# Two modulation groups of a diffusion-trunk kernel: from TensorE in the turnover to VectorE in the sub-layer before it

## The chip, the cores and the metric

One NeuronCore of a Trainium2 chip runs the whole program. The time is the device time of one execution in microseconds (us). Engines go by the profile's names: PE is TensorE (PEld its weight loads), DVE is VectorE, ACT is ScalarE, POOL is GpSimd, SP is SyncE, whose queue issues nearly all loads.

## The reference, cut to what matters

Two layers of a trunk, each of three sub-layers: SwiGLU, a token mixer, SwiGLU. Both token groups (128 prompt tokens, 256 latent tokens) go through all six sub-layers with shared weights. Every sub-layer is normed before and after and modulated by nine vectors a layer:

```
def adaln(cond, w, b):
    return (jax.nn.silu(cond) @ w + b)[:, None, :]
def pre_norm(x, mod, j, g):
    return rmsnorm(x, g) * (1 + mod_chunk(mod, 3 * j + 1)) + mod_chunk(mod, 3 * j)
def post_residual(x, out, mod, j, g, w):
    return x + w * mod_chunk(mod, 3 * j + 2) * rmsnorm(out, g)
def swiglu(h, w_in, w_out):
    gate, up = jnp.split(h @ w_in, 2, axis=-1)
    return (jax.nn.silu(gate) * up) @ w_out
```

`mod` is `silu(cond)` (two rows: prompt and latent) times a 1024 x 9216 matrix per layer, all float32. So there are 18 modulation groups of 1024 columns; sub-layer b uses groups 3b (shift), 3b+1 (scale) and 3b+2 (gate). D_MODEL is 1024, the inner width of SwiGLU 2816.

## The kernel before, in words

**Layout.** All activations stand transposed, features on the partitions, the 384 tokens in the columns: 8 tiles of 128x384 for the model width (KD = 8), 22 for the inner width. Every float32 product of the main matrices is made of three float32r matmuls (high x high, low x high, high x low), so each weight half of 1024x128 is split by ACT (WH, L394) and then by DVE (WL, L408) into its high and low part. Four such halves fit (the ring of WH and WL), and PE multiplies one after the other: `pe_half` (L439 to L441), 24 matmuls a half.

**The sub-layers.** Sub-layers 0 to 5 of the code (here: first to sixth) are ffn, even mixer, ffn, ffn, odd mixer, ffn. In an ffn, the in-phase takes 22 load slots of 256 columns (`in{s}`), the out-phase 12 (`out{s}`). Loads come in the order written out by `ring_order` (L129), six slots of 1 MB in RAW; SP waits until the slot's last user is done (`wait_ring`).

**The turnover.** Between two sub-layers PE sums squares over the partitions (L1616), DVE and ACT turn the sums into two scale rows, PE spreads them over the partitions (L1623, into bank 4 and bank 5), and then, for each of the 8 feature tiles, DVE scales the output (L1140), adds it to X (L1144), scales X (L1093) and takes the low part HL (L1107), with ACT giving the high part HH (L712) and the full one (L718). PE begins the next sub-layer with `pe_four` (L443 to L474): the first four halves at once, one feature tile after the other, each tile waiting for its HL. The first tile's eight matmuls on HH are L452 and L453, its four on HL L456, the other tiles L461 to L463, the last tile L470 to L472.

**Where the modulation groups come from.** A group is four load slots. There are two ways to compute one:

- On PE (`mod_pair`, L1536): 128 matmul records a group, straight from RAW, L1546, into a bank of its own. The turnover into sub-layer s+1 has one such group, named by `BETWEEN`: its first pair of slots is cut in pieces around the spread into bank 5, its second pair runs partly before and partly inside `first_four` (between the first and the second feature tile). After it ACT copies the rows out (`mod_rows_out`, L656, at the end of the turnover on ACT), PE transposes them (`mod_turn`, L1578, after the first four halves), ACT copies the columns (`mod_cols_out`, L661) and DVE adds bias and gain (`coefficients`, L1051).
- On DVE (`mod_sums`, L1079 and L1082): 16 multiply-add instructions of 128x256 a slot into SUMS or PARTS, within an ffn named in `SUMMED` (first, third and fourth sub-layer). PE then reduces each slot over the partitions with four matmuls between two halves (`mod_reduce`, L1600, 8 records), and for every two slots transposes a row (`sum_turn`, L1610, 2 records). Ten slots fall in the in-phase, those beyond ten in the out-phase after the output slots of `SUMMED_OUT` = (0, 1, 3, 4, 6, 7).

Before, the first sub-layer sums 4 groups (16 slots, six of them in its out-phase), the third and the fourth 3 groups each (12 slots, two of them in the out-phase).

Of the kernel before, what the change touches and what calls it, by code (L numbers as in the profile page):

```python
# [63 lines left out]

BETWEEN = ("modB", "modD", "modE", "modH", "modJ")
MOD_GROUPS = {"mod0": 2, "modA": 4, "modB": 1, "modC": 1, "modD": 1, "modF": 3, "modE": 1, "modG": 3, "modH": 1,
              "modJ": 1}


# [29 lines left out]


OPEN_BANK = (7, 6, 4, 7)
MOD_BANK = {6: 6, 7: 5, 8: 6, 12: 6, 16: 6, 17: 6}

IN_SLOTS = {"ffn": 22, "even": 16, "odd": 12}
OUT_SLOTS = {"ffn": 12, "even": 4, "odd": 4}
# [24 lines left out]
def ring_order():  # L132

    def run(st, a, b):
        return [(st, n) for n in range(a, b)]

    order = run("mod0", 0, 2) + run("in0", 0, 2) + run("mod0", 2, 8)
    for s in range(6):
        kind = SUBLAYERS[s][0]
        if s:  # L140
            order += run(f"in{s}", 0, 2) + run(BETWEEN[s - 1], 0, 4)
        if kind == "even":
            order += run(f"in{s}", 2, 6) + run("modC", 0, 2) + run(f"in{s}", 6, 7) + run("modC", 2, 4)
            order += run(f"in{s}", 7, 16) + run(f"out{s}", 0, 4)
        elif s in SUMMED:
            order += run(f"in{s}", 2, 4)
            for q in range(SUMMED_IN):
                order += run(f"in{s}", 2 * q + 4, 2 * q + 6) if q < 9 else run(f"out{s}", 0, 2)
                order += run(SUMMED[s], q, q + 1)
            for n in range(10):  # L150
                order += run(f"out{s}", n + 2, n + 3)
                q = SUMMED_IN + SUMMED_OUT.index(n) if n in SUMMED_OUT else None
                order += run(SUMMED[s], q, q + 1) if q is not None and q < summed_slots(s) else []
        else:
            order += run(f"in{s}", 2, IN_SLOTS[kind]) + run(f"out{s}", 0, OUT_SLOTS[kind])
    return order
# [23 lines left out]
def trunk(nc, x_prompt, x_sample, c, state_hgrn, cache_k, cache_v, c_ctx, mod_w, mod_b, norm_pre, norm_post,  # L180
# [5 lines left out]
    with ctx:  # L186
# [127 lines left out]
        rstd_done = sem("rstd_done")  # L314
# [306 lines left out]
        def _(act):  # L621
# [138 lines left out]
            def turnover(s, OUT, n):  # L760

                st = f"out{s}"
                nxt = ahead(act, split_act, s, "out", n)
                out_tile(s, OUT, st, n, 0, 6)
                nxt[0]()
                tile_squares(s, st, n, 1, 7)
                nxt[1]()
                if s == 5:
                    x_rows_out(0)
                    x_rows_out(1)  # L770
                    tile_scaled(s, OUT, 7)
                    root(sum_out(bank[0], 0), 0, (stat_done, 2 * s + 1))
                    for at in range(2, 2 * TOKS):
                        x_rows_out(at)
                    return
                root(sum_out(bank[0], 0), 0, (stat_done, 2 * s + 1))
                act.wait_ge(xy_done, 8 * s + 8)
                tile_scaled(s, OUT, 7)
                root(STAT[:, 4, :], 5, (sum_step, 5 * (s + 1)))
                high_parts(s + 1, 2)  # L780
                mod_rows_out(between(s + 1))

            def ffn(s):
                f, st = SUBLAYERS[s][1], f"in{s}"

                def pair(i, j):
                    nxt = [split_act(act, st, j + 2 + q, 8, i) for q in range(2)] if j < 20 else \
                        [split_act(act, f"out{s}", q, 8) for q in range(2)]
                    base = 22 * f + j
                    for b in range(2):  # L790
                        nxt[0][b]()
                        act.wait_ge(half_used, i * 12 + used(st, j, b))
                        act.wait_ge(gated, i * 6 + (base + b + 1))
                        act.activation(TT[:, b, :], cols3(bank[b]), ACT.Silu).then_inc(silu_done, 1)
                    nxt[1][0]()
                    nxt[1][1]()
                    for b in range(2):
                        act.wait_ge(gated, i * 6 + (2 + base + b + 1))
                        act.activation(AH[:, bass.ds(i * 6 + (j + b), 1), :], TT[:, 2 + b:3 + b, :],  # L799
                                       ACT.Copy).then_inc(act_hi, 1)  # L800
                    if s in SUMMED and j in (6, 10, 14, 18):
                        summed_rows_out(s, (j - 6) // 4)
                    if s in SUMMED and j in (8, 12, 16, 20):
                        summed_cols_out(s, (j - 8) // 4)

                ffn_pairs(act, pair, lambda: s and mod_cols_out(between(s)))
                for n in range(11):
                    for half in ahead(act, split_act, s, "out", n):
                        half()
                    if n == 0:  # L810
                        act.activation(STAT[:, 7, 1:2], EPSC[:], ACT.Sqrt)
                    if n in ROWS_OUT and 2 * ROWS_OUT[n] < summed_slots(s):
                        summed_rows_out(s, ROWS_OUT[n])
                    if n in COLS_OUT and 2 * COLS_OUT[n] < summed_slots(s):
                        summed_cols_out(s, COLS_OUT[n])
                    if n % 3 == 2:
                        for b in range(2):
                            out_tile(s, OUTF, f"out{s}", n, b, 2 * (n // 3) + b)
                turnover(s, OUTF, 11)
# [158 lines left out]
            def odd(s):  # L978
                for tau in range(24):
                    if tau % 2 == 0:  # L980
                        for half in ahead(act, split_act, s, "in", tau // 2):
                            half()
                    d = tau % 8
                    if tau < 16:
                        act.wait_ge(half_used, used(f"in{s}", tau // 2, tau % 2))
                        dst = (CB if tau < 8 else CG)[:, d, :]
                        for g, (t0, t1) in enumerate(GROUPS):
                            a = act.activation(dst[:, t0 + 1 + g:t1 + 1 + g], bank[tau % 4][:, t0:t1], ACT.Copy)
                        a.then_inc(proj_out, 1)
                    if tau == 3:  # L990
                        mod_cols_out(between(s))
                for d in range(KD):
                    act.wait_ge(conv_done, d + 1)
                    if d == 0:
                        act.wait_ge(half_used, used(f"in{s}", 11, 1))
                    for g, (t0, t1) in enumerate(GROUPS):
                        a = act.activation(HH[:, d, t0:t1], CG[:, d, t0 + 1 + g:t1 + 1 + g], ACT.Copy)
                    a.then_inc(cat_hi, 1)
                for n in range(3):
                    for b in range(2):  # L1000
                        ahead(act, split_act, s, "out", n)[b]()
                        out_tile(s, OUTC, f"out{s}", n, b, 2 * n + b)
                turnover(s, OUTC, 3)
# [19 lines left out]
        def _(dve):  # L1023
# [174 lines left out]
            def ffn(s):  # L1198
# [25 lines left out]
                    if s in SUMMED and j == 14:  # L1224
                        coefficients(first_group(SUMMED[s]))

                ffn_pairs(dve, pair, lambda: s and coefficients(between(s)))
                for n in range(11):
                    for half in ahead(dve, split_dve, s, "out", n):
                        half()  # L1230
# [194 lines left out]
            def odd(s):  # L1425
# [13 lines left out]
                for tau in range(24):  # L1439
                    if tau % 2 == 0:  # L1440
                        for half in ahead(dve, split_dve, s, "in", tau // 2):
                            half()
                    if tau == 3:
                        coefficients(between(s))
                    if tau < 16:
                        continue
                    d = tau - 16
# [73 lines left out]
        def _(pe):  # L1521
# [60 lines left out]
            def mod_reduce(s, q):  # L1582

                n0, k = summed_before(s) + q, q // 2
                if q % 2 == 0:
                    if n0 >= 4:
                        pe.wait_ge(sum_cols, n0 // 2 - 1)
                    if q == 0:
                        pe.wait_ge(out_done, 4 + 8 * s)
                    if q == 0 and s == 0:  # L1590
                        pe.wait_ge(open_cols, 4)
                    if q == 2 and s:
                        pe.wait_ge(mod_cols, between(s) + 1)
                    if q == SUMMED_IN:
                        pe.wait_ge(gated, 2 + 22 * SUBLAYERS[s][1] + 22)
# [31 lines left out]
            def first_four(s):  # L1627
# [6 lines left out]
                next(steps)  # L1634
                if s == 0:
                    open_turn(1)
                if s:
                    mod_pair(BETWEEN[s - 1], 2, range(2 if SUBLAYERS[s - 1][0] == "ffn" else 5, KD))
                for kk, _ in enumerate(steps, 1):
                    if s == 0 and kk in (1, 3):  # L1640
# [34 lines left out]
            def turnover(s):  # L1675
# [24 lines left out]
                     lambda t: sum_at(t, 0), closes=True).then_inc(stat_done, 1)  # L1700
                pe.wait_ge(rstd_done, 2 * s + 2)
                spread(bank[4], 1)
                st = BETWEEN[s]
                pe.wait_ge(out_done, 4 + 8 * s + 7)
                mod_pair(st, 0, range(early, early + 3))
# [5 lines left out]
            def ffn(s):  # L1711
# [17 lines left out]
                        if b == 0 and j in (8, 12, 16, 20) and s in SUMMED:  # L1729
                            sum_turn(s, (j - 8) // 4)  # L1730

                ffn_pairs(pe, pair, lambda: s and mod_turn(between(s)))
                st = f"out{s}"

                def quarter_pair(i, jj):
# [235 lines left out]

            def odd(s):
                first_four(s)
                mod_turn(between(s))
                for tau in range(4, 24):
                    if tau >= 20:
                        pe.wait_ge(conv_step, 4 * (tau - 20) + 1)
# [50 lines left out]
```

## Time and profile before

| what | us |
|---|---|
| median of 3 runs (1646.82 to 1647.25) | 1646.87 |
| the profiled execution, own time | 1645.01 |
| its span, first to last instruction | 1643.2 |
| PE busy | 1593.4 (97%) |
| DVE busy | 1067.7 (65%) |
| ACT busy | 693.2 (42%) |
| mean granted TensorE clock | 0.997 |

The page's engine table shows how busy an engine is over the whole program; which engine sets the time of a stretch is read from the chain of waits and from the timeline of the stretch. A matmul's record is longer than the step to the next one, since matmuls overlap. Durations of the timeline are of merged runs of equal instructions where a count stands behind.

### The profile page before, as it was taken

What the parts mean: (1) busy time and instruction counts of PE and PEld (TensorE: products, weight loads), DVE (VectorE), ACT (ScalarE), POOL (GpSimd) and SP (SyncE); (2) the same over time, 40 slices, a digit from 0 to 9 for tenths busy, and PEclk for the clock granted to TensorE, in tenths of its full rate; (3) what the DMA queues carried; (4) which work ended last, traced back from release to release, by engine and by line L of the source; (5) the groups of instructions that cost most, each with busy time, mean ns of one, the idle gap of its engine ahead of it and who ended that gap; (6) DMA issues with size and microseconds to landing.
All of it is one profiled execution on the core that took longest, in us unless ns stands there. A gap on an engine that the chain in (4) does not pass through costs nothing.

```text
span 1643.2 us, 25603 instructions
## 1 busy us (share of the span) xinstructions
PE 1593.4 (97%) x10383; PEld 1535.1 (93%) x10383; DVE 1067.7 (65%) x1950; ACT 693.2 (42%) x1228; POOL 42.1 (3%) x48
## 2 busy tenths in 40 slices
PE   5999999999999999999999999999999999999999
PEld 4999999988778989999999999999999999999999
DVE  5677778773568887777764777776472776343332
ACT  3433334463563466333343633333463356333333
POOL 2000000001100000000000000000000000000000
PEclk8999999999999999999999999999999999999999
DMA  9765556566221235555554655555363335333321
GB/s 329 248 196 168 192 169 216 179 219 207 86 81 35 91 117 184 190 177 180 191 168 128 205 168 192 179 173 185 129 206 129 128 108 183 125 125 122 116 71 38
DMA packets 255685, 260.12 MB, mean 158 GB/s; under 512 B 6625, under 2 KB 253826, under 8 KB 255570
## 3 DMA queue, kind: packets, MB, share of 16 engines
q1 hardware_dynamic: 250528, 253.25, 47.7%
q0 software_dynamic: 928, 2.44, 0.6%
q10 hardware_dynamic: 4114, 2.84, 0.6%
q8 instruction: 80, 1.31, 0.3%
q14 instruction: 35, 0.29, 0.1%
HBM read 255.88 MB, written 2.62 MB: 157 GB/s over the span
## 4 chain that ended last, share of the span: by engine, by line
PE 86%; DVE 7%; ACT 3%; issue 2%; POOL 1%; DMA 1%; ACTq 0%; DVEq 0%; POOLq 0%
PE bank L439 25%; PE bank L441 25%; PE bank L440 25%; PE bank L461 1%; PE bank L1616 1%; PE bank L463 1%; PE bank L462 1%; ACT WH L394 1%; DVE X L1144 1%; PE bank L1600 1%; DVE HL L1107 1%; DVE WL L408 1%; DVE SUMS L1409 1%; POOL WL L408 1%; DMA MIX<-in_x_sample 1%
## 5 line engine op out<-in xcount | busy, mean ns | idle before, releaser
L408 DVE TENSOR_TENSOR WL<-RAW,WH 128x1024 fp32r<-128x1024 f32 (+1 forms) x335 | 400.5, 1198 | 470.4 <-ACT WH L394 469.8
L394 ACT ACTIVATE WH<-RAW 128x1024 fp32r<-128x1024 f32 (+1 forms) x344 | 357.7, 1044 | 623.8 <-PE bank L441 610.6
L439 PE MATMUL bank<-HH,WH 128*128 128x384 f32 x1664 | 565.9, 340 | 8.0 <-DVE WL L408 3.5
L440 PE MATMUL bank<-HL,WH 128*128 128x384 f32 x1664 | 559.7, 336 | 0.0
L441 PE MATMUL bank<-HH,WL 128*128 128x384 f32 x1664 | 559.7, 336 | 0.0
L439 PEld LDWEIGHTS bank<-HH,WH 128*128 128x128 f32 x1664 | 313.3, 188 | 16.6 <-issue 10.7
L440 PEld LDWEIGHTS bank<-HL,WH 128*128 128x128 f32 x1664 | 313.3, 188 | 0.0
L441 PEld LDWEIGHTS bank<-HH,WL 128*128 128x128 f32 x1664 | 313.2, 188 | 0.0
L439 PE MATMUL bank<-AH,WH 128*128 128x384 f32 x704 | 238.5, 339 | 0.0
L440 PE MATMUL bank<-AL,WH 128*128 128x384 f32 x704 | 236.8, 336 | 0.0
L441 PE MATMUL bank<-AH,WL 128*128 128x384 f32 x704 | 236.7, 336 | 0.0
L1082 DVE SCALAR_TENSOR_TENSOR SUMS<-RAW,COND,SUMS 128x256 f32<-128x256 f32 x420 | 176.2, 478 | 0.0
L439 PEld LDWEIGHTS bank<-AH,WH 128*128 128x128 f32 x704 | 132.5, 188 | 2.0 <-ACT OUTF L747 1.0
L440 PEld LDWEIGHTS bank<-AL,WH 128*128 128x128 f32 x704 | 132.6, 188 | 0.0
L441 PEld LDWEIGHTS bank<-AH,WL 128*128 128x128 f32 x704 | 132.5, 188 | 0.0
L799 ACT ACTIVATE AH<-TT 128x384 fp32r<-128x384 f32 x88 | 45.6, 519 | 108.8 <-DVE TT L1216 108.8
L461 PE MATMUL bank<-HH,WH 128*128 128x384 f32 x192 | 66.7, 347 | 4.5 <-DVE HL L1107 2.9
L463 PE MATMUL bank<-HH,WL 128*128 128x384 f32 x192 | 64.7, 337 | 0.0
L462 PE MATMUL bank<-HL,WH 128*128 128x384 f32 x192 | 64.6, 337 | 0.0
L712 ACT ACTIVATE HH<-TT,MOD,CA 128x128 fp32r<-128x128 f32 x96 | 47.3, 540 | 33.6 <-DVE TT L1093 32.1
L1082 DVE SCALAR_TENSOR_TENSOR PARTS<-RAW,COND,PARTS 128x256 f32<-128x256 f32 x140 | 56.3, 478 | 0.0
L1221 DVE TENSOR_TENSOR AL<-TT,AH 128x384 fp32r<-128x384 f32 x88 | 48.8, 554 | 5.5
(241 smaller groups left out, 1496.3 us busy)
## 6 DMA issues: line engine op xcount, KB each, us to landing
RAW<-in_ffn_w_in SPq DMA_DIRECT2D x88, 1024.0 KB, 5.1
RAW<-in_mod_w SPq DMA_DIRECT2D x72, 1024.0 KB, 5.1
RAW<-in_ffn_w_out SPq DMA_DIRECT2D x32, 1024.0 KB, 5.2
RAW<-in_ab_w_in SPq DMA_DIRECT2D x16, 1024.0 KB, 5.7
RAW<-in_ffn_w_out SPq DMA_DIRECT2D x16, 768.0 KB, 4.9
RAW<-in_cv_w_in SPq DMA_DIRECT2D x12, 1024.0 KB, 5.1
RAW<-in_ab_w_out SPq DMA_DIRECT2D x4, 1024.0 KB, 5.2
RAW<-in_cv_w_out SPq DMA_DIRECT2D x4, 1024.0 KB, 5.4
```

Source lines behind the costliest of these rows:

```text
L394: e.activation(WH[:, (2 * m + b) % 4, 0:nk, :], RAW[:, p, 0:nk, b * P:(b + 1) * P], ACT.Copy).then_inc(half_hi, 1)
L408: e.tensor_tensor(WL[:, k, 0:nk, :], RAW[:, p, 0:nk, b * P:(b + 1) * P], WH[:, k, 0:nk, :].bitcast(F32), ALU.subtract).then_inc(half_ready, 1)
L439: e.matmul(out, WH[:, k, kk, :], xh(kk), start=(first and kk == 0), stop=False)
L440: e.matmul(out, WH[:, k, kk, :], xl(kk), start=False, stop=False)
L441: mm = e.matmul(out, WL[:, k, kk, :], xh(kk), start=False, stop=(last and kk == nk - 1))
L461: e.matmul(outs[b], WH[:, kh[b], kk, :], HH[:, kk, :], start=False, stop=False)
L462: e.matmul(outs[b], WH[:, kh[b], kk, :], HL[:, kk, :], start=False, stop=False)
L463: e.matmul(outs[b], WL[:, kh[b], kk, :], HH[:, kk, :], start=False, stop=False)
L712: a = act.activation(HH[:, d, t0:t1], TT[:, d % 2, t0:t1], ACT.Identity, bias=MOD[:, 24 * s + d, g:g + 1], scale=CA[:, s, d, g:g + 1])
L799: act.activation(AH[:, bass.ds(i * 6 + (j + b), 1), :], TT[:, 2 + b:3 + b, :], ACT.Copy).then_inc(act_hi, 1)
L1082: x = dve.scalar_tensor_tensor(a[:, g, :], w, by, a[:, g, :], ALU.mult, ALU.add)
L1221: dve.tensor_tensor(AL[:, at, :], TT[:, 2 + b:3 + b, :], AH[:, at, :].bitcast(F32), ALU.subtract).then_inc(act_ready, 1)
```

## The change

`modE` (group 12) leaves the turnover from third to fourth sub-layer and becomes the fourth group of `modF`, summed in the third sub-layer; `modH` (group 16) leaves the turnover from fourth to fifth and becomes the fourth group of `modG`, summed in the fourth. `BETWEEN` becomes a dictionary of the turnovers that still have a group (0, 1 and 4), and everything that belongs to such a group is left out elsewhere. In these two turnovers PE then only sums and spreads.

```
-BETWEEN = ("modB", "modD", "modE", "modH", "modJ")
-MOD_GROUPS = {"mod0": 2, "modA": 4, "modB": 1, "modC": 1, "modD": 1, "modF": 3, "modE": 1, "modG": 3, "modH": 1,
+BETWEEN = {0: "modB", 1: "modD", 4: "modJ"}
+MOD_GROUPS = {"mod0": 2, "modA": 4, "modB": 1, "modC": 1, "modD": 1, "modF": 4, "modG": 4,
                "modJ": 1}
-MOD_BANK = {6: 6, 7: 5, 8: 6, 12: 6, 16: 6, 17: 6}
+MOD_BANK = {6: 6, 7: 5, 8: 6, 17: 6}
@@ ring_order
-            order += run(f"in{s}", 0, 2) + run(BETWEEN[s - 1], 0, 4)
+            order += run(f"in{s}", 0, 2) + (run(BETWEEN[s - 1], 0, 4) if s - 1 in BETWEEN else [])
@@ ACT, turnover
-                mod_rows_out(between(s + 1))
+                if s in BETWEEN:
+                    mod_rows_out(between(s + 1))
@@ ACT, ffn
-                ffn_pairs(act, pair, lambda: s and mod_cols_out(between(s)))
+                ffn_pairs(act, pair, lambda: s - 1 in BETWEEN and mod_cols_out(between(s)))
@@ ACT, odd
-                    if tau == 3:
-                        mod_cols_out(between(s))
@@ DVE, ffn
-                ffn_pairs(dve, pair, lambda: s and coefficients(between(s)))
+                ffn_pairs(dve, pair, lambda: s - 1 in BETWEEN and coefficients(between(s)))
@@ DVE, odd
-                    if tau == 3:
-                        coefficients(between(s))
@@ PE, mod_reduce
-                    if q == 2 and s:
+                    if q == 2 and s - 1 in BETWEEN:
@@ PE, first_four
-                if s:
+                if s - 1 in BETWEEN:
                     mod_pair(BETWEEN[s - 1], 2, range(2 if SUBLAYERS[s - 1][0] == "ffn" else 5, KD))
@@ PE, turnover
                 spread(bank[4], 1)
+                if s not in BETWEEN:
+                    pe.wait_ge(out_done, 4 + 8 * s + 7)
+                    pe.wait_ge(rstd_done, 2 * s + 3)
+                    spread(bank[5], 6)
+                    return
@@ PE, ffn
-                ffn_pairs(pe, pair, lambda: s and mod_turn(between(s)))
+                ffn_pairs(pe, pair, lambda: s - 1 in BETWEEN and mod_turn(between(s)))
@@ PE, odd
                 first_four(s)
-                mod_turn(between(s))
```

## Rows read from the trace of the kernel before

**Rows 1.** The page: the chain that ended last, shares of the span by engine.

```profile
PE 86%; DVE 7%; ACT 3%; issue 2%; POOL 1%; DMA 1%; ACTq 0%; DVEq 0%; POOLq 0%
```

**Rows 2.** Chain of waits, turnover to the fourth sub-layer: start, us, what.

```profile
905.68 0.10 DVE STAT L1087
...
912.44 0.55 DVE HL L1107
```

**Rows 3.** Timeline of PE, 903.9 to 914 us: start, us, instruction, idle before.

```profile
904.91 0.86 PE L1546 MATMUL bank<-RAW,COND 128*32 128x128 f32 x24
905.82 0.94 PE L1623 MATMUL bank<-IDENT,STAT 128*128 128x128 f32 x6
906.69 1.74 PE L1546 MATMUL bank<-RAW,COND 128*32 128x128 f32 x56
908.74 0.41 PE L452 MATMUL bank<-HH,WH 128*128 128x384 f32 x1 [0.32 <-ACT HH L712]
...
911.25 1.52 PE L1546 MATMUL bank<-RAW,COND 128*32 128x128 f32 x48
913.05 0.45 PE L461 MATMUL bank<-HH,WH 128*128 128x384 f32 x1 [0.27 <-DVE HL L1107]
```

**Rows 4.** Timeline of PE, turnover to the fifth sub-layer.

```profile
1207.74 0.44 PE L461 MATMUL bank<-HH,WH 128*128 128x384 f32 x1 [0.28 <-DVE HL L1107]
```

**Rows 5.** Timeline of all engines, end of the turnover, 918 to 934 us.

```profile
926.16 0.34 PE L472 MATMUL bank<-HH,WL 128*128 128x384 f32 x1
...
926.41 0.37 ACT L656 ACTIVATE ROWS<-bank 128x256 f32<-128x256 f32 x1
...
926.67 1.05 ACT L394 ACTIVATE WH<-RAW 128x1024 fp32r<-128x1024 f32 x1
...
927.90 0.51 PE L1578 MATMUL bank<-IDENT,ROWS 128*128 128x8 f32 x4
...
929.20 0.42 PE L439 MATMUL bank<-HH,WH 128*128 128x384 f32 x1 [0.80 <-DVE WL L408]
```

**Rows 6.** Chain of waits, end of the turnover to the fifth sub-layer.

```profile
1221.01 0.19 PE bank L472
...
1221.28 0.99 ACT WH L394
```

**Rows 7.** Timeline of PE, tenth reduction and first sums: first, then third sub-layer.

```profile
240.61 0.43 PE L1600 MATMUL bank<-SUMS,PICK 128*32 128x128 f32 x8
...
324.44 0.76 PE L1616 MATMUL bank<-ONES,SUMS 128*128 128x44 f32 x6
...
819.57 0.43 PE L1600 MATMUL bank<-SUMS,PICK 128*32 128x128 f32 x8
...
900.68 0.54 PE L1616 MATMUL bank<-ONES,SUMS 128*128 128x44 f32 x4
```

**Rows 8.** Busy time there: stretch, length, PE, PEld, DVE, ACT, POOL, clock, DMA.

```profile
240.60:324.40 83.80, 83.80 (x521) 80.91 (x521) 69.61 (x142) 32.98 (x64) 0.00 (x0) 1.00 0.62 201
819.40:900.70 81.30, 81.30 (x487) 80.04 (x486) 45.73 (x76) 32.54 (x60) 0.00 (x0) 1.00 0.48 156
```

**Rows 9.** Timeline of PE around one reduction, first sub-layer.

```profile
256.09 0.34 PE L440 MATMUL bank<-AL,WH 128*128 128x384 f32 x1
256.26 0.34 PE L441 MATMUL bank<-AH,WL 128*128 128x384 f32 x1
...
256.89 0.45 PE L439 MATMUL bank<-AH,WH 128*128 128x384 f32 x1
```

**Rows 10.** Timeline of PE in the opening.

```profile
21.04 0.94 PE L1623 MATMUL bank<-IDENT,STAT 128*128 128x128 f32 x6 [1.87 <-DVE STAT L1087]
...
27.35 3.64 PE L1561 MATMUL bank<-RAW,COND 128*32 128x128 f32 x64 [5.24 <-DMA RAW<-in_mod_w]
```

**Rows 11.** Stretches: the opening (columns of rows 8); fifth sub-layer, PE alone.

```profile
15.00:50.00 35.00, 27.27 (x326) 24.34 (x318) 25.43 (x52) 17.49 (x36) 10.85 (x6) 0.85 1.09 348
...
1306.50:1309.90 3.40, 0.77 (x5) 1.00 0.00 0
```

## The prediction

> **What bounds the kernel now.** I read the page's chain that ended last first: PE holds 86% of it [rows 1], so PE's time counts wherever PE doesn't wait. Where it does wait is then a question for each stretch that the change touches, and there are two kinds. In the out-phases of the first and third sub-layers PE is busy for every microsecond of the stretch, at the full clock, while DVE has 14 us or more free of 81 to 84 [rows 8]: there each instruction added to PE lengthens the program, and work added to DVE costs nothing as long as it fits. In the turnovers it is the other way round. PE's sums end, DVE and ACT make two scale rows, and then DVE's elementwise chain over the feature tiles sets the pace: the chain of waits goes through DVE's reciprocal, the spread, and DVE's instructions up to HL of the second tile [rows 2]. PE's timeline has the group's matmuls exactly in those waits: after the third block of them it still sits idle for 0.27 us until HL is there, after the second for 0.32 us until ACT has HH [rows 3]. The turnover to the fifth sub-layer ends in the same wait, 0.28 us [rows 4].
>
> **Taken out of the turnovers.** Per turnover, PE loses 24 + 56 + 48 = 128 records, 0.86 + 1.74 + 1.52 = 4.12 us [rows 3], and the transposition of the rows, 0.51 us [rows 5]: 4.63 us of PE work, 9.26 us for both. What of it lay on the path?
> - First block, 904.91 to 905.77: the spread behind it begins at 905.82 [rows 3], and DVE's reciprocal, whose piece of the chain ends at 905.78, lets it go [rows 2]. With the block gone the spread still begins at 905.82. Gain 0.
> - Second block, until 908.4: the next matmul waits for ACT's HH, with 0.32 us idle [rows 3]. Gain 0, and PE waits some 2 us instead.
> - Third block, until 912.77: the next matmul follows 0.06 us after HL ends (912.44 + 0.55 = 912.99) [rows 2, 3]. Gain 0. From there PE runs the remaining tiles without a further wait, as before. The same holds for the turnover to the fifth sub-layer by its own row [rows 4].
> - ACT's copy of the rows, 0.37 us, stands just ahead of the first split of the next half, on which PE waits 0.80 us at 929.20 [rows 5]. The copy is on the path in form, but that split also waits until PE has let go of the weights: PE's matmul ends at 926.16 + 0.34 = 926.50. In the other turnover, where ACT is idle before it, the split begins 0.08 us after such an end, at 1221.28 after 1221.01 + 0.19 [rows 6]. So it could begin at 926.58 and begins at 926.67 [rows 5]: I take a gain of 0.09 us, with bounds 0 and 0.37.
> - In the turnover to the fifth sub-layer the split is let go by PE itself [rows 6]; the removed copy of the rows was over before. Gain 0.
> - PE's transposition, 927.90 to 928.41, lies in the wait that ends at 929.20 [rows 5]: 0. ACT's copy of the columns and DVE's two small instructions come after it, beside PE's full halves: 0. If that cover went, they would cost under 1 us together.
> - SP: the four loads of each group leave the place between slots 2 and 3 of the next sub-layer, so the next weight slots come earlier; no split waits for a load there, before or after.
>
> **Put into the out-phases.** The third and fourth sub-layers get four more summed slots each, 12 to 15: four reductions and two transposed rows on PE, four slots of DVE work, four loads in SP's queue, one more group of coefficients. The first sub-layer already runs this very program with 16 slots, so its out-phase is the price list. From the tenth reduction to the first sums it takes 324.44 - 240.61 = 83.83 us, the third sub-layer takes 900.68 - 819.57 = 81.11 us [rows 7] (the fourth the same 81.11, by the same view). The difference is **2.72 us** for four reductions and two rows. As a cross-check, one reduction: between L441 and the next L439 lie 0.63 us where the step from L440 to L441 is 0.17 [rows 9], so 0.46, and the first matmul behind it is 0.1 us slow (0.45 us where the others take 0.34): 0.56. Four of these are 2.2 us, two rows take the rest, 0.25 us each.
>
> DVE gets 69.61 - 45.73 = 23.9 us more in each out-phase and then stands at 69.6 of 83.8 us [rows 8]. In the first sub-layer PE is busy for all of those 83.80 us, so the later splits are still in time; the loads too, which SP issues behind the same waits for DVE. The last slot is summed after the eighth of twelve output slots, well ahead of the turnover. If DVE's cover were gone, each late split would show as a wait of PE's L439 for L408.
>
> **The sum.** 2 x 2.72 - 0.09 = **+5.35 us**. For the profiled execution that is 1645.01 + 5.35 = 1650.4; the median of before stands 1.86 us above that execution (1646.87), so the median becomes **1652.2 us**, +0.33%. Bounds: the removed work returns between 0 and 0.37 us for ACT's copy, and up to 0.3 us a turnover if PE's idle between matmul blocks also held up the waiting matmul; on the other side a first matmul after idle takes 0.41 to 0.45 us instead of 0.34 [rows 3], two or three times a turnover, up to 0.3 us. With one of the two ends at a time that gives 1651.3 (5.35 - 0.28 - 0.6) to 1652.9 (5.35 + 0.09 + 0.6).
>
> **Rivals.**
> - **Faster: the group's matmuls did hold up PE.** The place is the turnover; if the waits shown after the blocks are only the time in which a full queue of small matmuls runs empty, then all 4.63 us leave the path and 2.72 come back: -1.91 each, 1646.87 - 3.8 = 1643.1 us. It decides from the point where PE's step before L461 shortens with nothing ahead of it, that is, if more than 2.72 of the 4.63 us were exposed. Against it: in both turnovers the matmul starts 0.05 to 0.1 us after DVE's HL ends [rows 2, 3], and DVE waits for nothing of PE's there but the spreads. 5%.
> - **The same: about half is hidden.** If the turnovers give back over 1 us each, or the reductions fall into waits, the sum stays below 3.3 us: about 1649. The first sub-layer's 2.72 us speak against it; what speaks for it is only that four small instructions may be placed luckier. 7%.
> - **The clock falls.** In the new turnover PE works 0.94 us, waits 2 us, works 2 us on the first tile, and waits 1.8 us. In the opening PE had waited 1.87 us, run a spread of 0.94 us and begun a wait of 5.24 us [rows 10] when the granted clock fell to 1.2 GHz; the mean of 0.85 over 35 us [rows 11] makes 35 x 0.15 / 0.5 = 10.5 us at the low level. Once per turnover this costs up to 5.2 us less the 1.8 us that PE would have waited: some 3.4 to 5.2 each, 1659 to 1663 us in all. Against it: around the 2.99 us hole of the fifth sub-layer PE was busy for 0.77 of 3.40 us and kept the full clock [rows 11], and the new turnover is busier than that. 6%.
> - **DVE comes late** in the fuller out-phases, or SP's loads do. Each late split costs up to its own 1.2 us; with one per added slot, 8 x 1.2 = 9.6, about 1661 us. The first sub-layer's full PE row [rows 8] speaks against it. 3%.
> - That the change doesn't do what it says (matmuls left in the turnovers) I hold for excluded by the diff: the calls are behind the new conditions.
>
> [...]
>
> **Numbers.** Forecast 79%, clock 6%, DVE 3%, same 7%, faster 5%. A measurement of this kernel can tell about 0.2%, 3.3 us, from no change. Faster 0.05; same 0.09 (the case and the low tail of the forecast); slower 0.86. The range takes the forecast's bounds, a microsecond for the gap between the profiled execution and the median, and a part of the neighbouring cases on both sides: 1649.8 to 1655.0.
>
> **What would show it.** In the profile of after: no L1546 and L1578 in these two turnovers; first sums to the first L439 as long as before within 0.1 us (900.68 to 929.20 us in the first of them [rows 5, 7]); waits of the spread L1623, L452 and L461 longer, with DVE and ACT as releasers; tenth reduction to first sums 83.8 us in the third and fourth sub-layers, DVE at 70 us there; clock 1.00 throughout. I am wrong if the turnovers shorten by more than 0.5 us each, if L439 waits for L408 in the out-phases, or if the clock column shows less than 1.00 there.

## The result

The changed kernel takes 1653.44 us (median of 7 runs, 1650.59 to 1653.55) against 1646.82 before: ratio 1.0039, 95% interval 1.0028 to 1.0049. It is slower by 6.6 us, 0.40%. Of the seven runs of the kernel before, one took 4680.29 us; the other six lie between 1645.08 and 1647.25 us, and without it their median would be 1646.81. The forecast was 1652.2 us in a range of 1649.8 to 1655.0, and slower with a chance of 0.86.

The page of the changed kernel (1652.87 us for the profiled execution, 7.9 us over that of before): PE has 192 instructions less and as much busy time, DVE 47.6 us more.

```profile
span 1651.1 us, 25359 instructions
...
PE 1594.7 (97%) x10191; PEld 1534.5 (93%) x10191; DVE 1115.3 (68%) x2078; ACT 693.5 (42%) x1232; POOL 42.2 (3%) x48
```

The out-phase of the third sub-layer, from the windows view of the changed kernel (columns as in [rows 8]). It now reads like the first sub-layer's of before: 83.80 us, PE busy in all of it, DVE at 69.

```profile
820.50:904.30 83.80, 83.80 (x521) 80.89 (x521) 69.34 (x141) 32.99 (x64) 0.00 (x0) 1.00 0.62 202
```

The turnover behind it on PE, from the timeline of the changed kernel. It answers to [rows 3]: from the first spread to the second, to the first tile and to the second tile the steps are as before to 0.1 us, and where the group's matmuls were PE is idle, 0.93, 1.98 and 1.72 us. New is what comes next: L461, 0.34 us long before, takes 0.52 us in the two rows ahead of the last.

```profile
907.72 0.94 PE L1620 MATMUL bank<-IDENT,STAT 128*128 128x128 f32 x6
909.59 0.91 PE L1620 MATMUL bank<-IDENT,STAT 128*128 128x128 f32 x6 [0.93 <-DVE STAT L1086]
912.47 0.42 PE L452 MATMUL bank<-HH,WH 128*128 128x384 f32 x1 [1.98 <-ACT HH L712]
...
916.78 0.44 PE L461 MATMUL bank<-HH,WH 128*128 128x384 f32 x1 [1.72 <-DVE HL L1106]
...
918.27 0.52 PE L461 MATMUL bank<-HH,WH 128*128 128x384 f32 x1
919.23 0.52 PE L461 MATMUL bank<-HH,WH 128*128 128x384 f32 x1
...
934.27 0.42 PE L439 MATMUL bank<-HH,WH 128*128 128x384 f32 x1 [1.07 <-DVE WL L408]
```

The clock column says why. Windows of 2 us in the changed kernel (the column behind POOL is the granted clock, share of full speed): it falls to 0.50, that is 1.2 GHz, within 916 to 918 us, when the second tile's matmuls (from 916.78) have just begun, and is back between 920 and 922; in the next turnover it falls between 1210 and 1212.

```profile
914.00:916.00 2.00, 1.05 (x5) 0.65 (x4) 1.93 (x6) 0.58 (x2) 0.00 (x0) 1.00 0.01 4
916.00:918.00 2.00, 1.22 (x6) 1.22 (x7) 1.93 (x5) 1.71 (x4) 0.00 (x0) 0.88 0.03 8
918.00:920.00 2.00, 2.00 (x8) 2.00 (x7) 1.93 (x5) 1.75 (x5) 0.00 (x0) 0.50 0.00 0
920.00:922.00 2.00, 2.00 (x11) 2.00 (x10) 1.97 (x4) 1.75 (x5) 0.00 (x0) 0.77 0.00 0
...
1210.00:1212.00 2.00, 0.92 (x3) 0.92 (x4) 1.87 (x5) 0.98 (x2) 0.00 (x0) 0.76 0.91 313
1212.00:1214.00 2.00, 2.00 (x8) 2.00 (x7) 1.97 (x6) 0.98 (x2) 0.00 (x0) 0.50 0.03 8
```

Where the 7.9 us between the two profiled executions lie, by the first sums (L1616, L1613 in the changed kernel) and the first L439 behind them in each timeline:

| stretch | before | after | difference |
|---|---|---|---|
| start to the first turnover's sums | 324.44 | 324.59 | +0.15 |
| from there to the second turnover's sums (even mixer) | 281.10 | 281.90 | +0.80 |
| from there to the third turnover's sums | 295.14 | 297.86 | +2.72 |
| third turnover, first sums to first L439 | 28.52 | 29.92 | +1.40 |
| from there to the fourth turnover's sums | 266.18 | 268.89 | +2.71 |
| fourth turnover, first sums to first L439 | 28.44 | 28.51 | +0.07 |
| from there to the end of the span | 419.4 | 419.4 | 0.0 |

The out-phases bring 5.43 us, the turnovers 1.47. Both bare turnovers had a stretch of 3.4 us at the low clock, and yet one cost 1.40 us and the other 0.07. In the third turnover the low stretch fell on the second and third feature tile, behind which PE has no wait in which to make the time good. In the fourth it fell on the first tile, and that tile has a wait behind it: PE waits 0.61 us for the second tile, where it waited 1.72 us in the third turnover, and the rest goes on as before.

```profile
1211.08 0.69 PE L452 MATMUL bank<-HH,WH 128*128 128x384 f32 x1 [1.78 <-ACT HH L712]
...
1215.59 0.44 PE L461 MATMUL bank<-HH,WH 128*128 128x384 f32 x1 [0.61 <-DVE HL L1106]
```

The 0.80 us of the even mixer, which the change doesn't touch, goes with the clock too: it was low between 524 and 530 us in this execution and not in the one of before. In a row of 21 runs of the kernel before the mean clock read 0.995 to 0.997 and the time 1645.3 to 1648.8 us. So the kernel before probably has such falls as well, though its one profile shows none behind the opening.

### The profile page after: what moved, and what is told of

Read it like the earlier page. It is cut to its first block, busy times and chain, and to the rows that moved or that the text cites. A ratio compares the mean times of both kernels' runs of the same rounds, so it can differ in the third digit from the quotient of the medians.

```text
span 1651.1 us, 25359 instructions
## 1 busy us (share of the span) xinstructions
PE 1594.7 (97%) x10191; PEld 1534.5 (93%) x10191; DVE 1115.3 (68%) x2078; ACT 693.5 (42%) x1232; POOL 42.2 (3%) x48
## 4 chain that ended last, share of the span: by engine, by line
PE 87%; DVE 6%; ACT 2%; issue 2%; DMA 1%; SPq 1%; DVEq 0%; ACTq 0%
PE bank L439 25%; PE bank L441 25%; PE bank L440 24%; PE bank L461 1%; PE bank L462 1%; PE bank L463 1%; PE bank L1613 1%; PE bank L1597 1%; ACT WH L394 1%; DMA RAW<-in_mod_w 1%; SPq L532 1%; DVE X L1143 1%; PE bank L1911 1%; DVE WL L408 1%; DVE SUMS L1408 1%
## 5 line engine op out<-in xcount | busy, mean ns | idle before, releaser
L439 PE MATMUL bank<-HH,WH 128*128 128x384 f32 x1664 | 566.2, 340 | 8.6 <-DVE WL L408 3.7
L441 PE MATMUL bank<-HH,WL 128*128 128x384 f32 x1664 | 559.8, 336 | 0.0
L439 PEld LDWEIGHTS bank<-HH,WH 128*128 128x128 f32 x1664 | 313.3, 188 | 17.7 <-issue 11.2
L441 PEld LDWEIGHTS bank<-HH,WL 128*128 128x128 f32 x1664 | 313.2, 188 | 0.0
L439 PE MATMUL bank<-AH,WH 128*128 128x384 f32 x704 | 239.6, 340 | 0.0
L441 PE MATMUL bank<-AH,WL 128*128 128x384 f32 x704 | 236.7, 336 | 0.0
L439 PEld LDWEIGHTS bank<-AH,WH 128*128 128x128 f32 x704 | 132.4, 188 | 3.6 <-ACT OUTF L747 1.8
L441 PEld LDWEIGHTS bank<-AH,WL 128*128 128x128 f32 x704 | 132.4, 188 | 0.0
L1081 DVE SCALAR_TENSOR_TENSOR PARTS<-RAW,COND,PARTS 128x256 f32<-128x256 f32 x252 | 101.3, 478 | 0.0
L461 PE MATMUL bank<-HH,WH 128*128 128x384 f32 x192 | 67.2, 350 | 6.2 <-DVE HL L1106 4.7
```

The lines of the kernel that those rows point to most:

```text
L439: e.matmul(out, WH[:, k, kk, :], xh(kk), start=(first and kk == 0), stop=False)
L441: mm = e.matmul(out, WL[:, k, kk, :], xh(kk), start=False, stop=(last and kk == nk - 1))
L461: e.matmul(outs[b], WH[:, kh[b], kk, :], HH[:, kk, :], start=False, stop=False)
L1081: x = dve.scalar_tensor_tensor(a[:, g, :], w, by, a[:, g, :], ALU.mult, ALU.add)
```

## The experiments

Medians against runs of the kernel before on the same chip. The kernel before had 1646.8 us beside all of them, but 1646.0 beside the last two.

**1. Filler in the two bare turnovers.**

```
+            def fill(n):
+                for kk in range(n):
+                    for strip in range(4):
+                        pe.matmul(bank[6][32 * strip:32 * strip + 32, 0:P], COND[:, kk % KD, :], ONES[:],
+                                  start=True, stop=True)
...
                     pe.wait_ge(out_done, 4 + 8 * s + 7)
+                    fill(3)
                     pe.wait_ge(rstd_done, 2 * s + 3)
                     spread(bank[5], 6)
+                    fill(7)
                     return
...
+                elif s:
+                    fill(6)
```

> The changed kernel with filler in the two turnovers without a group: 12, 28 and 24 matmuls (24, 56 and 48 records, as many as the group had there) of constant data into bank 6, whose results nobody reads. Theory: the changed kernel loses 2 x 2.7 us in the out-phases and a further 1 to 2 us because the granted clock falls for a few us in the bare turnovers. Then the filler keeps the clock at 1.00 there, the turnover to the fourth sub-layer (first sums to first L439) goes back from 29.92 to about 28.5 us, and the median lands at 1652.2 us, 1 to 1.4 below the changed kernel's 1653.4. Rival, the longer turnover comes from something else that left with the group (order of the loads, ACT's start): it stays at 29.9 us and the median at 1653.4. Rival, small matmuls hold PE up: over 1654.

Measured: 1652.08 us, ratio 1.0029 (1.0017 to 1.0040). The turnovers take 28.45 and 28.46 us. The padded kernel stands 5.32 us over the one of before, where the sum of the prediction had 5.35. The median is 1.4 us under the changed kernel's, but the intervals of the two overlap, and the padded runs lie in three groups (two near 1650.5, three near 1652.1, two near 1653.4); what the clock cost is read from the turnover, 29.92 against 28.45 us, with the clock at 1.00 in it. This execution lost 2.9 us elsewhere, in the odd mixer: PE waits 2.99 us there, as before, and this time the clock fell in that hole and stayed low for 6.8 us. The rows are from the padded kernel's timeline and from its windows (length, PE busy, clock):

```profile
1315.88 0.66 PE L452 MATMUL bank<-HH,WH 128*128 128x384 f32 x1 [2.99 <-issue]
1316.34 0.52 PE L453 MATMUL bank<-HH,WL 128*128 128x384 f32 x1
```

```profile
1314.00:1316.00 2.00, 0.12 (x1) 0.81 0.01 4
1316.00:1318.00 2.00, 2.00 (x7) 0.50 0.73 230
1318.00:1320.00 2.00, 2.00 (x8) 0.50 0.86 294
```

**2. The group's matmuls taken away, nothing added.** The kernel before, with a quarter of the matmuls of these two groups.

```
-                for kk in steps:
+                for kk in [k_ for k_ in steps if st not in ("modE", "modH") or k_ in (0, KD - 1)]:
```

> The kernel before with the matmuls of groups 12 and 16 cut to the first and last of the eight feature tiles (32 records instead of 128 in each of the two turnovers); it leaves out three quarters of the products of these two groups. Theory: nothing is won in the turnovers, which stay at 28.5 us where the clock stays, and become up to 1.5 us longer where it falls; median 1646.8 to 1648.5 us. Rival, the group's matmuls were partly exposed: 0.5 to 1.5 us a turnover less, median 1644 to 1646.

Measured: 1646.62 us, ratio 0.9997 (0.9988 to 1.0006); the turnovers take 28.52 and 28.46 us, to 0.02 us as before. Three quarters of 4.12 us of PE work can leave a turnover and nothing is won, so the group was hidden. (In this kernel's profile the clock was low in the third turnover from 909 to 913 us, while PE ran the first tile; PE was through with it just as the second tile's HL was there, so it cost nothing.) The rival by which it was exposed falls.

**3. The added reductions taken away, DVE's work kept.**

```
+                if s and q >= 12:
+                    pe.sem_inc(mod_reduced, 1)
+                    return
                 e = PICK[:, 1 - q % 2:33 - q % 2]
```

> The changed kernel without the matmuls of the eight added reductions (slots 12 to 15 of the third and the fourth sub-layer); DVE's sums, the loads and the transposed rows stay. It leaves out the reduction over the partitions of half of groups 11, 12, 15 and 16. Theory: the out-phases' cost is PE's alone, 0.56 us a reduction: tenth reduction to first sums 81.6 us instead of 83.8 in both sub-layers, median 4.5 us under the changed kernel, 1648.9. Rival, DVE's 24 us or the four added loads per sub-layer hold PE up: the stretch stays above 83 us and the median above 1652.

Measured: 1648.22 us, 5.2 us under the changed kernel's 1653.44 and 0.7 under what was expected. The windows view of this kernel: DVE carries the same 69 us, and the stretch is down at 81.6, as expected to the tenth.

```profile
820.00:901.60 81.60, 81.60 (x489) 80.42 (x489) 69.19 (x141) 32.99 (x64) 0.00 (x0) 1.00 0.63 207
```

From 901.68 - 820.09 = 81.59 us against 83.82 with them, four reductions cost 2.23 us, 0.56 each; what is left over 81.11 are the two rows, 0.24 each. DVE's added 24 us and the four loads cost nothing.

**4. Half as many interruptions, the same matmuls.** The kernel before, with two slots reduced at once.

```
-            t = SUMS if q < SUMMED_IN else PARTS
-            return t[:, 512 * (q % 2):512 * (q % 2) + 512].rearrange("p (c n) -> p c n", c=2)
+            if q >= SUMMED_IN:
+                t, at = PARTS[:], 512 * (q - SUMMED_IN)
+            elif q % 3 == 2:
+                t, at = SQ[:, :, :].rearrange("p a b -> p (a b)"), 0
+            else:
+                t, at = SUMS[:], 512 * (q % 3)
+            return t[:, at:at + 512].rearrange("p (c n) -> p c n", c=2)
...
-                    if n0 >= 2:
-                        dve.wait_ge(mod_reduced, n0 - 1)
+                    if n0 >= 3 and q < SUMMED_IN:
+                        dve.wait_ge(mod_reduced, n0 - 2)
...
+                if q % 2 == 0:
+                    return
...
+                for r in range(2):
+                    e, a = PICK[:, 1 - r:33 - r], partial(s, q - 1 + r)
+                    for strip in range(4):
+                        mm = pe.matmul(sum_bank(k)[32 * strip:32 * strip + 32, 0:P], e,
+                                       a[:, strip % 2, strip // 2 * P:strip // 2 * P + P], start=(r == 0),
+                                       stop=(r == 1))
+                mm.then_inc(mod_reduced, 2)
```

> The kernel before with its reductions done two at a time, at the place of every second one (a third buffer in SQ for the in-phases, six in PARTS for the out-phases): the same matmuls, 20 interruptions of PE instead of 40. Theory: an interruption costs 0.2 us of its own beside the 0.36 us of its eight records (and 16 records in a row take less than twice 0.36), so each merged pair saves 0.2 to 0.3 us: median 4 to 6.4 us under 1646.8, 1640.4 to 1642.8. Rival, the cost lies in the matmuls: no saving, 1646.5 or more; or DVE waits for its buffers and PE for DVE: over 1648.

Measured: 1640.36 us, ratio 0.9959 (0.9945 to 0.9972), 6.4 us faster than before and 0.04 us under the lower end of what was expected. The timeline of this kernel, first sub-layer, beside [rows 9]: from L441 to L439 there are 0.84 us for 16 records, where 8 records took 0.63.

```profile
238.78 0.34 PE L441 MATMUL bank<-AH,WL 128*128 128x384 f32 x1
239.04 0.42 PE L1606 MATMUL bank<-SQ,PICK 128*32 128x128 f32 x8
239.29 0.40 PE L1606 MATMUL bank<-SUMS,PICK 128*32 128x128 f32 x8
239.62 0.44 PE L439 MATMUL bank<-AH,WH 128*128 128x384 f32 x1
```

With 0.1 us for the slow matmul behind it a merged pair costs 0.84 - 0.17 + 0.1 = 0.77 us, two single reductions 1.12. So by these rows 0.21 of the 0.56 us of a reduction are its matmuls and 0.35 is the interruption. The whole stretches give a little less: from the second turnover's sums to the third's the merged kernel takes 293.22 us against 295.14, and six pairs stand in it, 0.32 us each, which is also what the median gives (6.4 us for 20). What the interruption consists of no run here shows.

**5. The same in the changed kernel.** The same edit on the changed kernel, 24 merged pairs.

> The changed kernel with its reductions done two at a time (48 slots, 24 interruptions of PE instead of 48). Merging won 6.4 us in the kernel before with 20 merged pairs, 0.32 us a pair. Theory: 24 x 0.32 = 7.7 us under the changed kernel's 1653.4, 1645.7 us; the bare turnovers still lose 1 to 2 us to the clock, so it stays about 5 us above the merged kernel before (1640.4), less 4 x 0.32 = 1.3: 1644.4 to 1646. Rival, the clock falls no more: 1644 or less.

Measured: 1644.43 us, ratio 0.9987 (0.9978 to 0.9996). It lies at the lower edge of the expectation: 9.0 us under 1653.44, and 4.1 over the merged kernel of before, where 2 x 2.72 - 4 x 0.32 = 4.2 is the out-phases' part alone (4.0 with 0.35). That leaves nothing for the clock, while this kernel's profile shows one fall that made the fourth turnover 29.86 us; medians of kernels whose runs spread over 3 us (here 1642.9 to 1646.0) don't settle a microsecond.

**6. The reductions put where the group had been.** The changed kernel, merged, with slots 10 to 15 of the third and fourth sub-layer reduced in the bare turnover and their rows and columns taken as the group's were.

```
                     pe.wait_ge(out_done, 4 + 8 * s + 7)
+                    mod_reduce(s, 11)
                     pe.wait_ge(rstd_done, 2 * s + 3)
                     spread(bank[5], 6)
+                    mod_reduce(s, 13)
+                    mod_reduce(s, 15)
                     return
...
+                late = s in LATE and q > SUMMED_IN
+                B, at = (bank[6], P * (k - 5)) if late else (sum_bank(k), 0)
...
+                    if d == 1 and s - 1 in LATE:
+                        dve.wait_ge(mod_reduced, summed_before(s))
                     low(s, d - 1)
```

> The same, and the six slots of the out-phases of the third and the fourth sub-layer (10 to 15) are reduced in the bare turnover instead: one pair between the two spreads, two pairs after the second one, into bank 6, their rows copied and transposed where the group's were before. Theory: PE waits there anyway (0.93, 1.98 and 1.8 us), so all six reductions and three rows of a sub-layer leave the path: tenth reduction to first sums falls from 83.8 to about 79.4 us (81.11 less two reductions and one row, 1.3 to 1.7 us), the turnover stays at 28.5 us plus what the clock takes, at most 0.3 more for ACT's longer copy. Median 1638.5 to 1641, under both kernels and at or below the merged kernel before. Rival, DVE's wait for the reductions ahead of the first HL, or ACT's copy, makes the turnover as much longer: 1643 or more.

Measured: 1638.05 us, ratio 0.9948 (0.9934 to 0.9961). From the reduction to the first sums it is now 895.38 - 815.64 = 79.74 us, and the turnovers take 28.57 and 29.73 us. The first of them, from this kernel's timeline: 48 records of reductions, and still PE waits 0.27 and 0.92 us. From the second turnover's sums to the third's it takes 292.15 us, 1.07 less than the merged kernel before (experiment 4), and from the third turnover's end to the fourth's sums 1.04 less. What is still empty is the gap ahead of the second tile, and there the clock fell in the other turnover (1198 to 1200 us, windows view): the last row of the first view is from there.

```profile
899.61 0.65 PE L1638 MATMUL bank<-PARTS,PICK 128*32 128x128 f32 x16
900.52 0.94 PE L1671 MATMUL bank<-IDENT,STAT 128*128 128x128 f32 x6 [0.27 <-DVE STAT L1115]
901.39 1.08 PE L1638 MATMUL bank<-PARTS,PICK 128*32 128x128 f32 x32
903.39 0.42 PE L453 MATMUL bank<-HH,WH 128*128 128x384 f32 x1 [0.92 <-ACT HH L736]
...
1199.47 0.69 PE L462 MATMUL bank<-HH,WH 128*128 128x384 f32 x1 [1.71 <-DVE HL L1135]
```

```profile
1196.00:1198.00 2.00, 1.60 (x8) 1.00 0.00 0
1198.00:1200.00 2.00, 0.53 (x2) 0.84 0.01 4
1200.00:1202.00 2.00, 2.00 (x8) 0.50 0.03 8
```

**7. The same with filler in the gaps that remain.**

```
+                elif s:
+                    fill(6, 7)
...
+                pe.wait_ge(out_done, 8 * s + 4)
+                fill(10, 4)
                 for _ in out_four(s, range(KD), lambda kk: pe.wait_ge(cat_ready, 8 + kk + 1)):
```

Here the filler writes the last 128 columns of its bank, bank 7 in the turnovers and bank 4 in the hole; so it does in experiment 8, in bank 4.

> The same again with filler on PE (constant data, nobody reads it) in the waits that are left: 48 records between the first and the second feature tile after the two turnovers, 80 records in the 3 us hole ahead of the odd mixer's output projection. Theory: the granted clock falls no more in these three places, which takes 1 to 3 us and most of the scatter out: median 1637 to 1638.5, runs within 1.5 us. Rival, the late reductions already keep the clock up and the odd mixer's hole is harmless: same as the run without filler within 0.5 us.

Measured: 1636.74 us, ratio 0.9939 (0.9926 to 0.9953), and five runs within 0.16 us (1636.63 to 1636.79). I had expected 1637 to 1638.5, so the time came 0.3 us lower. The turnovers take 28.57 and 28.40 us. This is the fastest kernel of the study, 10.1 us under the one of before and 16.7 under the first median of the change. Its filler stands in the timeline where PE waited before, and the tile behind it comes as soon as HL is there:

```profile
905.97 1.52 PE L1590 MATMUL bank<-ONES,COND 128*32 128x128 f32 x48
907.76 0.44 PE L462 MATMUL bank<-HH,WH 128*128 128x384 f32 x1 [0.28 <-DVE HL L1135]
```

**8. Filler in the odd mixer's hole alone, in the kernel before.** The last two added lines of the diff above, on the kernel before.

> The kernel before with 80 filler records in the 3 us hole ahead of the odd mixer's output projection, and nothing else. Theory: some executions of the kernel before lose up to 2.9 us because the granted clock falls in that hole (a run of the padded kernel showed it); with the filler none does: median 1645.2 to 1646 against 1646.8, highest run under 1647. Rival, its scatter comes from elsewhere (the even mixer): no difference within 0.3 us; or the filler delays the first matmul: up to 1648.

Measured: 1645.24 us, ratio 0.9991 (0.9982 to 1.0000), runs from 1645.08 to 1645.84, where 21 runs of the kernel before beside it went from 1645.3 to 1648.8. The median gain of 1.5 us is below what a measurement of this kernel can tell with certainty; what is plain is that the runs above 1646 us, most of those of the kernel before, are gone.

**9. and 10. The change with its clock kept, and as it is.** First the changed kernel with the filler of experiment 1 in the turnovers and 80 records in the odd mixer's hole as in experiment 8, then the changed kernel itself beside it.

> The changed kernel with filler in both bare turnovers (as in the padded kernel) and 80 filler records in the odd mixer's 3 us hole, so that the clock stays up in all three places. Against the kernel before with its hole filled (1645.24 us) only the out-phases' additions are left. Theory: 2 x 2.72 us, so 1650.6 us, runs within 1 us. Rival, something beside the clock and the out-phases was in the change: off by more than 0.5 us.

> The changed kernel as it is, beside the one before on this list and on the same chip. Theory: 1652 to 1653.6 us as before, 1.5 to 3 us above the filled one, with runs spread over 2 us or more.

Measured: 1650.52 us (seven of eight runs from 1650.38 to 1651.27, the eighth 1651.52), ratio 1.0028 (1.0017 to 1.0039), and 1651.32 us (1650.48 to 1652.91), ratio 1.0034 (1.0022 to 1.0046). The first is 5.28 us over the filled kernel before of experiment 8, which was measured in another batch; 5.35 was the sum. Its runs spread over 1.1 us, a little more than expected. The second missed its expectation: it came 0.7 us under it and only 0.8 us over the padded one. In its profile the third turnover took 29.89 us again and the fourth 28.53, with the clock at 0.70 between 916 and 918 us. But three of its six runs, 1650.48 to 1650.62 us, are as fast as the padded kernel's, so in those executions the bare turnovers seem to have cost next to nothing. In this batch the changed kernel stands 5.3 us over the 1646.0 of the kernel before, which the out-phases fill alone. So what the bare turnovers cost differs from execution to execution, and the medians say no more than between nothing and 1.4 us.

## Why the prediction was right, and which term was off

**The out-phases, 2 x 2.72 us: right to 0.01 us.** The first sub-layer of the kernel before was the price list, and the third and fourth now read 2.71 and 2.71 us more. Experiment 3 splits it: 0.56 us a reduction, 0.24 a row. The cross-check from [rows 9] had 0.56 and 0.25.

**DVE's 24 us and SP's loads, nothing: right.** PE is busy in all of the 83.80 us after, as in [rows 8], and experiment 3 keeps DVE's work and drops PE's cost. The rival of a late DVE falls. (Its price, added to the forecast of 1652.2, is 1661.8 us and not 1661.)

**The group's 9.26 us on PE, nothing won: right.** Experiment 2 takes most of the matmuls away and the turnovers stay to 0.02 us. The faster rival falls with it.

**ACT's copy, 0.09 us: right in size, and too small to tell.** With the clock kept up (experiments 1 and 9) the third turnover takes 28.45 and 28.46 us against 28.52, and the fourth, for which no gain was forecast, 28.46 and 28.47 against 28.44.

**The clock: the step that failed.** The prediction put the turnovers at no loss and gave the rival of the falling clock 6%, with 3.4 to 5.2 us a turnover. Among its signs it named a clock of 1.00 throughout, and that one wasn't met. The clock did fall: in both bare turnovers of the changed kernel's two profiles and of experiment 3's, and in one of the two in experiment 5's. What was mis-sized is the price: the term was worked out from a low stretch of 10.5 us in the opening, and the low stretches here lasted 3.4 us, in experiments 3 and 5 once 6.8 us, and where they met the first tile the wait behind it took up most of the loss. They cost 1.40 and at most 0.07 us in the profiled execution, and 0.67 and at most 0.07 in that of experiment 3. I had set the chance low because of one hole of 2.99 us through which the clock had held [rows 11]. That was one draw: the same hole cost 2.9 us in experiment 1. In the turnover with the cost the clock fell after waits of 0.93, 1.98 and 1.72 us with a spread and one tile's matmuls between them. The Trainium skill's page "TensorE: Matmul & The Clock Gate" ("Why this matters for your kernels") warns only of single idle gaps between bursts that are longer than any of these waits; here page and trace differ, and the measurement decides.

So of the 6.6 us 5.4 are interruptions in PE's full stretches, shown by experiment 3 and by the filled kernels. The 1.2 us that are left fit the clock's falls in the turnovers, but as a figure for the median they aren't shown: in the second batch the difference was 5.3 us and nothing was left. The forecast came 1.2 us under the first median and 0.9 over the second, and that both lie in the range is partly luck: it reached toward the neighbouring cases, and the clock had not been priced well.

## What to carry to other kernels

Work that stands in another engine's wait is free even on the busiest engine; moving it to an idle engine is a loss if the busy one must then be interrupted in a full stretch, be it for 8 small records. Before moving such work ask which stretch will pay, and put its PE part back into the gap: here that took 6.4 us off the changed kernel (experiment 5 to experiment 6) and left it some 2 us ahead of the kernel before with the same merging (experiment 4). Merging the interruptions alone won 6.4 us. Where one program has two versions of a stage, read the price of the change off the other one.

## What the runs showed of the hardware that I had not expected

- An interruption of a stream of 128x384 matmuls by eight records with 128 columns costs 0.56 us and one by sixteen records 0.77, so that 0.35 us is the same for both (0.32 by the whole stretches).
- The granted clock fell to 1.2 GHz in turnovers in which PE was never idle for more than 1.99 us at a time (experiment 3; 1.98 in the changed kernel), and held or fell in one and the same hole of 2.99 us from one execution to the next (1.00 in the kernel before; 0.81 over its end and 0.50 from 1316 us on in experiment 1). One profile without a fall says little about the next execution.
- Much of this kernel's scatter goes with this clock. With filler in three places five runs lay within 0.16 us, without it (experiment 6) within 1.55 us. Constant data whose result nobody reads was enough as filler, and it cost nothing where PE would have waited.
